# The mixer norm's gain transfer: from the head of SyncE's queue to ScalarE's queue

## The reference

```python
def _rmsnorm(x, g):
    xf = x.astype(jnp.float32)
    y = xf * lax.rsqrt(jnp.mean(xf * xf, axis=-1, keepdims=True) + EPS)
    return (y * g.astype(jnp.float32)).astype(x.dtype)
...
    for l in range(DEPTH):
        h = _rmsnorm(x, norm_mix_g[l])
        proj = h @ w_in[l]
        a_val, a_gate, b_in = jnp.split(proj, [D_CONV, 2 * D_CONV], axis=-1)
        ya = _conformer_conv_mixer(a_val, a_gate, conv_a_w[l], conv_a_b[l],
                                   ln_a_g[l], ln_a_b[l])
        yb = _multiscale_pool_mixer(b_in, pool_w[l], pool_scale[l])
        x = x + jnp.concatenate([ya, yb], axis=-1) @ w_out[l]
        h = _rmsnorm(x, norm_ffn_g[l])
        gate, val = jnp.split(h @ w_up[l], 2, axis=-1)
        gate = _causal_dwconv(gate, conv_f_w[l], conv_f_b[l])
        x = x + (jax.nn.silu(gate) * val) @ w_down[l]
    return _rmsnorm(x, norm_final_g)
```

## Time and profile before

| | us |
|---|---|
| median of 3 runs | 910.6 |
| lowest and highest | 909.83, 910.98 |
| the profiled execution, own time | 909.48 |
| its span, first to last instruction | 907.5 |
| TensorE matmul busy | 889.1 (98% of the span) |
| VectorE busy | 706.4 |
| GpSimd busy | 674.7 |
| ScalarE busy | 417.6 |
| all transfers, share of 16 DMA engines (main queue) | 19.9% |

### The profile page before, as it was taken

How to read it: one execution, slowest core, us unless ns; L and a number is a source line. 1 busy time by engine, 2 the same in 40 slices (tenths; PEclk the granted TensorE clock), 3 DMA queues, 4 the chain that set the end, 5 groups by cost and what they waited for, 6 DMA issues and landing times.

```text
span 907.5 us, 11212 instructions
## 1 busy us (share of the span) xinstructions
PE 889.1 (98%) x4004; PEld 735.8 (81%) x4004; DVE 706.4 (78%) x755; ACT 417.6 (46%) x640; POOL 674.7 (74%) x505
## 2 busy tenths in 40 slices
PE   7999999999999999999999999999999999999996
PEld 6888887788888888888888888888888888888875
DVE  7799999996697895876858768587685876858667
ACT  8666655863564542433424434244342433424335
POOL 3679998683179896977959779597795977959822
PEclk9999999899999999999999999999999999999999
DMA  9321012051001112111121211312113121130114
GB/s 294 107 80 47 1 47 72 23 163 47 1 5 43 58 39 90 47 59 47 44 84 40 67 47 35 93 35 70 46 37 93 31 75 37 46 93 20 35 63 186
DMA packets 62997, 57.73 MB, mean 64 GB/s; under 512 B 2170, under 2 KB 56158, under 8 KB 62942
## 3 DMA queue, kind: packets, MB, share of 16 engines
q1 hardware_dynamic: 62942, 57.01, 19.9%
HBM read 52.81 MB, written 4.19 MB: 63 GB/s over the span
## 4 chain that ended last, share of the span: by engine, by line
PE 88%; DVE 7%; ACT 3%; issue 2%; DMA 0%; POOL 0%; DVEq 0%; SPq 0%; ACTq 0%; POOLq 0%
PE slot L2287 86%; DVE slot L1647 3%; PE slot L2319 1%; ACT junk L961 1%; DVE w_lo L1612 1%; DVE slot L1941 1%; ACT prod L961 1%; DMA x_sb<-in_x 0%; DVE act_lo L1740 0%; DVE shift L1715 0%; DVE bn L1699 0%; PE slot L2561 0%; ACT act_hi L970 0%; ACT std L964 0%; PE slot L2395 0%
## 5 line engine op out<-in xcount | busy, mean ns | idle before, releaser
L751 POOL TENSOR_TENSOR ring<-raw,ring 128x512 fp32r<-128x512 f32 x200 | 275.3, 1395 | 106.1 <-ACT ring L1154 106.0
L1154 ACT ACTIVATE ring<-raw 128x512 fp32r<-128x512 f32 x204 | 120.8, 624 | 221.7 <-POOL raw L774 97.0
L2287 PE MATMUL slot<-act_hi,ring 128*128 128x512 f32 x680 | 219.8, 389 | 0.0
L1955 DVE TENSOR_TENSOR x_sb<-x_sb,slot 128x1024 f32<-128x1024 f32 x140 | 169.3, 1216 | 59.8 <-PE slot L2287 54.7
L2287 PE MATMUL slot<-sums,ring 128*128 128x512 f32 x780 | 186.9, 389 | 0.0
L2287 PEld LDWEIGHTS slot<-sums,ring 128*128 128x128 f32 x780 | 146.5, 188 | 30.3
L2287 PEld LDWEIGHTS slot<-act_hi,ring 128*128 128x128 f32 x680 | 127.7, 188 | 26.4
L713 POOL TENSOR_TENSOR conv<-conv,prod 128x512 f32<-128x512 f32 (+9 forms) x89 | 121.8, 1390 | 23.0 <-ACT prod L1076 16.2
L2287 PE MATMUL slot<-act_lo,ring 128*128 128x512 f32 x340 | 132.3, 389 | 0.0
L774 POOL TENSOR_TENSOR raw<-raw 128x512 f32<-128x512 f32 x88 | 121.7, 1383 | 13.1 <-POOL ring L751 3.4
L1647 DVE SCALAR_TENSOR_TENSOR slot<-x_sb,chan_head,slot 128x512 f32<-128x512 f32 (+16 forms) x143 | 102.1, 740 | 2.7
(11 more groups left out here) (200 smaller groups left out, 1465.2 us busy)
## 6 DMA issues: line engine op xcount, KB each, us to landing
raw<-in_w_up SPq DMA_DIRECT2D x44, 256.0 KB, 2.9
raw<-in_w_up SPq DMA_DIRECT2D x22, 512.0 KB, 3.9
raw<-in_w_down SPq DMA_DIRECT2D x22, 512.0 KB, 3.2
x_sb<-in_x SPq DMA_DIRECT2D x12, 512.0 KB, 6.3
raw<-in_w_in SPq DMA_DIRECT2D x4, 1024.0 KB, 5.2
raw<-in_w_out SPq DMA_DIRECT2D x4, 1024.0 KB, 4.9
out<-raw SPq DMA_DIRECT2D x7, 512.0 KB, 2.7
raw<-in_w_in SPq DMA_DIRECT2D x4, 512.0 KB, 8.3
```

The source lines that it names most:

```text
L751: nc.gpsimd.tensor_tensor(block_at(n, 1), block_raw(n), block_at(n, 0).bitcast(F32), ALU.subtract).then_inc(block_lo, 1)
L1154: nc.scalar.activation(block_at(n, 0), block_raw(n), ACT.Copy).then_inc(block_hi, 1)
L1955: nc.vector.tensor_tensor(dst, dst, slot[part_slot(i, p)][:, :].rearrange("p (a n) -> p a n", a=2), ALU.add).then_inc(part_added, 1)
L2287: mm = nc.tensor.matmul(out_ap, st[s], mv[v], start=first and s == v == 0, stop=last and s == 1, skip_group_check=onto)
```

## The change

The transfer of `gain_part` is taken out of SyncE's stream, where it was the first issue, and put at the head of ScalarE's stream, ahead of the wait for the small constant and of the warming Sqrt. Its source, destination and semaphore are the same.

```diff
@@ -592,7 +592,6 @@
                 sp.dma_start(raw[:, 1, kk * SEQ:(kk + 1) * SEQ], w_down_v[:, 2 * i + kk, :])\
                   .then_inc(down_loaded[kk], 16)
 
-            sp.dma_start(gain_part[:, :], norm_mix_g.rearrange("a (p c) -> (a p) c", p=P)).then_inc(gain_part_loaded, 16)
             for m in range(HT):
                 load_x(m)
             load_half(0, 0)
@@ -987,6 +986,7 @@
                 nc.scalar.activation(half_of(w_hi[s][:, :], columns, t),
                                      half_of(raw[:, q % 2, :], columns, t), ACT.Copy).then_inc(hi_done, 1)
 
+            act.dma_start(gain_part[:, :], norm_mix_g.rearrange("a (p c) -> (a p) c", p=P)).then_inc(gain_part_loaded, 16)
             act.wait_ge(small_ready, 1)
             nc.scalar.activation(warm[:, :], eps[:, :], ACT.Sqrt)
```

## The result

The changed kernel takes 914.7 us (median of 6 runs, 913.3 to 915.68) against 909.9 for the kernel before (6 runs, 909.35 to 910.98): a ratio of 1.0049, 95% interval 1.0039 to 1.0059. It is 4.8 us slower. The forecast was 910.2, range 909.0 to 911.9, with 0.88 on no change. The profiled execution took 914.52, its span is 912.5, 5.0 more than the span of before.

The account below looks back on a forecast made before the run. TensorE's matmuls fill 98% of the span, so only the opening could move: -0.43 us from x issued earlier, ScalarE's issue and the gain's landing hidden. Against the 910.6 median this gave 910.2 us, range 909.0 to 911.9.

Parts of the forecast that it names:

- the two chains: Opening: x through ScalarE to TensorE, without slack; beside it the gain's data through TensorE and VectorE, with 1.29 us of slack.
- the x chain: SyncE's queue, one issue fewer: tile 0 and everything behind it start and land earlier, -0.43 us.
- rival 2: ScalarE's stream: table load placed ahead of the gain transfer, D at least 1.29, change at least 0.00, up to +1.28; chance 0.07.
- ScalarE's idle time: ScalarE before tile 0 lands: 2.76 us idle covers the added issue, cost nothing; without the cover 0.37 us.
- D: How much later than 2.37 us the gain lands; taken between 0 and 0.86, upper bound 1.71.
- rival 1: DMA: issues one after the other or packets interleaved, D 0.9 to 1.7, change -0.4 to +0.4 us; chance 0.24.
- the formula: Opening, ScalarE's take-up of tile 0: change is the larger of -0.43 and D - 1.29; taken as -0.43 us.
- the sum: Whole kernel: -0.43 us for the earlier x, added issue free, gain hidden; 910.6 - 0.43 = 910.2.
- Rival 5: TensorE's granted clock: the 0.50 stretch from 158 to 166 us lengthens or shortens, some 2 us either way; chance 0.05.
- Rival 3: DMA: gain queued behind the backlog of x, lands at 8.34, D = 5.97, change +4.7 us, 915.3; chance 0.07.

Follow-up runs that it names:

- Experiment 3: The changed kernel, with GpSimd waiting for the four normed tiles before its first low weight part; 910.84 us, ratio 1.0011.
- experiment 6: The changed kernel, with the gain's 4 KB laid out as 8 rows of 512 bytes and spread by products instead of transposes; 913.69 us, ratio 1.0045.
- experiment 8: The kernel before with 40 instead of 16 filling transposes, 912.12 us; the same with GpSimd waiting for the four normed tiles, 910.82 us.
- experiment 5: The kernel before with the gain issued second on SyncE's own queue, behind tile 0 of x; 913.53 us, ratio 1.0037.
- experiment 6's control: The kernel before, gain first on SyncE's queue, with the gain in 8 rows of 512 bytes; 912.56 us, ratio 1.0028.
- experiment 1: The kernel before, with tile 0 of x issued from ScalarE and the gain still first on SyncE; 913.41 us, ratio 1.0034.
- experiment 4: The changed kernel, with 18 more filling transposes on TensorE ahead of tile 3's transposes; 912.34 us, ratio 1.0027.
- experiment 7: The changed kernel with the gain in 8 rows and 4 instead of 16 filling transposes, 913.65 us; with GpSimd waiting for four normed tiles too, 912.69.

## Why the prediction was wrong, step by step

**Right.** The views and the two chains; the gain of the x chain is real, but it was 0.29 us in the profile and not 0.43 (first square at 4.70, not 4.56): x was issued 0.43 earlier and took 3.94 instead of 3.80 to land. The table load stood behind the transfer (rival 2 fell), and it was covered by ScalarE's idle time.

**The step that failed first: D.** I took D between 0 and 0.86, "nearest to the one row of this very transfer", with an upper bound of 1.71. It was 4.89 - 2.37 = 2.52. The row I leaned on was of the gain alone on idle DMA engines; the condition that the change removes is just that. The mechanism of rival 1, packets in turn, was right, and its size wrong. The DMA queues of the changed kernel from 3.0 to 3.5 and from 3.5 to 4.0 us (packets, MB, share):

```profile
q1 hardware_dynamic: 42, 0.17, 84.0%
q10 hardware_dynamic: 44, 0.00, 5.0%
...
q1 hardware_dynamic: 62, 0.20, 98.9%
q10 hardware_dynamic: 61, 0.00, 6.8%
```

One small packet for one of x, in both stretches. In the kernel before, 133 packets of the gain moved in the quarter of a microsecond from 1.75 to 2.0. I had let the turns begin at 1.7; on ScalarE's queue the first gain packets move only after 2.25, behind the first ones of x, and x's rate is still climbing then, so that a turn costs more than the 0.16 us of full rate. The Trainium skill's page DMA: Bandwidth & Descriptors, section Issuing engines are not separate DMA queues, is borne out: transfers of both engines interleave on the same 16. Its section Queues, rings and completion order, by which an engine drains some 9 to 17 descriptors of one queue before it changes, is not: by the prediction's estimate from that rule D would have been under 0.2, and the packets counted here come in equal numbers from both queues, one for one.

**The step that failed worst: the formula.** For D = 2.52 "the larger of -0.43 and D - 1.29" gives +1.23, and the take-up of tile 0 by ScalarE did move by nearly that much, 1.12, from 10.48 to 11.60 (before, the first normed tile had waited for its reciprocal, which ended at 6.67, and not for the gain's copy, so the gain had a little more slack than I gave it). Experiment 3, with the gain as late and the rest undone, costs 0.9 us. The other 3.9 us are a step that the sum didn't have. It took each instruction's duration from the kernel before as a constant and only moved the starts. But VectorE's normed tile and GpSimd's weight part can't run together. The Trainium skill, page SBUF — State Buffer, section Who interferes with whom, says that a VectorE instruction with two SBUF inputs contends with a GpSimd instruction that reads SBUF, that the shared pair of ports is an exclusive lock, and that issue order decides who blocks. The traces agree: GpSimd at 13.22 holds for 2.36, to 15.58, and the tile ends 1.08 later, at 16.66.

**Why it is a tie and not bad luck.** While x sets ScalarE's pace, GpSimd's start (12.09) comes 1.19 us after VectorE's (10.90). Once ScalarE waits for tile 0's transposes, both hang on the same event. From tile 0's start on VectorE at 9.06, VectorE reaches its fourth tile after three of its periods (1.40, 1.39, 1.39) at 13.24; the other way goes by tile 0's transposes (end 11.56), ScalarE's two instructions (11.60, 12.09) and GpSimd's start at 13.22. Two sums, 4.18 and 4.16, equal by the accident of the durations. The program ties the two in a second way. `tmp` has room for two tiles, so VectorE's third tile waits for the transposes of the first, the same event that ScalarE waits for:

```python
                if row == IN and m >= 2:

                    dve.wait_ge(pe_done, J_T1[m - 2] + 1)
```

In experiment 6 this wait is the one that counts: ScalarE takes tile 0 up at 10.93 and GpSimd starts 1.63 later; VectorE's third tile starts at 11.13 and its fourth 1.40 later, so 12.56 and 12.53. A delay of tile 0's transposes by much more than 1.3 us leads to this tie whatever its cause (experiments 6 and 8 with the gain in time), unless x is late as well, as in experiment 5. The order within 0.03 us decides, and the trace's stamps don't resolve it: in experiment 6 VectorE is stamped 0.03 ahead and loses.

**The clock.** Rival 5 was argued away with "its cause moves with everything else". The old stretch at 0.50 did move along, at a difference of 0.45 us; behind the tie came a new one. After 2.46 us without work TensorE did its filling at the 1.2 GHz level: 3.45 us to the first product instead of 1.94, another 1.5. The wait alone doesn't bring it about: in experiment 6's control 2.51 us without work cost nothing of the kind. What decides is open.

**The account for the profiled execution**, to the first product: 1.32 from the late gain (experiment 3's 1.10 in the start of the filling, plus the 0.22 by which the gain was later here than there), 2.15 from the tie, 1.51 from the clock; 4.98 in all, which is the measured 21.16 - 16.18. The sum closes because 2.15 is what the other two leave; that it is the tie is checked by the 2.14 us that the fourth tile took too long.

**The shape of the rivals.** Rival 3 had the sign, and its price of +4.7 even the size, but by another mechanism: I put its threshold for 0.2% at D = 3.11. With the tie the threshold lies lower, between D = 1.29 (experiment 1, no tie) and D = 2.11 (experiment 4, tie), and the cost beyond it jumps by 2 to 4 us at once, without or with the clock. Of 0.09 for slower, that is where the missing chance was.

## What to carry to other kernels

A small transfer of many small packets should be issued before the large ones or land with slack to spare: its landing time alone on idle DMA engines says nothing of its landing beside a bulk load. A sum of shifts holds only as long as no two instructions that exclude each other change their order; before trusting it, list the pairs of VectorE and GpSimd instructions near the chain and how far apart they start. Where such a pair stands in a tie, one semaphore wait that fixes the order costs next to nothing, and in experiments 3 and 8 it took away a whole level of the times. It didn't in experiment 7: there may be more than one such pair.

## What the runs showed of the hardware

- Packets of 32 bytes on one queue and of 4 KB on another alternate one for one (44 to 42, 61 to 62); 4 KB of gain then took 4.1 us to land instead of 1.6. In 8 packets they landed at 2.18 and 2.16 us beside the same load, and at 3.00 in a third trace.
- It did not matter which of the two engines issued: alone from ScalarE the gain landed at 2.55.
- A GpSimd instruction 0.02 us ahead held up VectorE for 2.14 us; 0.06 us behind it in experiment 8, or 0.11 in experiment 1, it paid 1.1 us itself (3.46 and 3.42 instead of 2.36). One stamped 0.03 us behind, in experiment 6, held VectorE up all the same.
- The same kernel can lose such a tie in one execution and win it in the next: seven of eleven against four by the times of experiment 8, where one that was won is traced and the wait removes the upper level.
- After 2.46 and 2.51 us without work the granted clock was 0.50 in two traces and stayed at 1.00 in a third (2.51).
